# Dilated attention in halves of four heads between projections, and latent prompt attention with V stationary and probabilities scaled ahead of the turn

## The chip, the cores and the metric

The kernel runs on one core of one Trainium2 chip. The metric is the device time of one execution in microseconds, the median of several runs. Everything is computed in 32-bit floats, so each matrix multiplication shows as two passes (MATMUL records) on TensorE, and a turn (transpose by the identity) as one.

## The reference, cut to what matters

One step of a decoder trunk with two layers, for a prompt of 1024 tokens and for 8 new tokens that each have 8192 cached positions. The first layer mixes with latent attention and gated linear attention, the second with dilated attention; each is followed by a SwiGLU FFN, and each sublayer by a LayerNorm. The change is in the prompt part of the latent attention and in the whole of the dilated attention.

```
def mla_attend(q_lat, q_pe, kv, q_pos):               # latent attention, 8 heads, causal
    s = (q_lat . c_kv + q_pe . k_pe) * (64 + 32) ** -0.5
    p = softmax(where(k_pos <= q_pos, s, -inf))
    return p . c_kv                                    # then times w_uv: 64 values a head

def odd_mixer(x, bufs, w_in, w_out):                   # 3 groups (window, dilation) x 8 heads x 64
    qkv = x @ w_in
    for g, (window, dil) in enumerate(((128, 1), (512, 4), (2048, 16))):
        o_g, lse_g = attention in blocks of 128 positions of equal residue, with ALiBi bias
        rows_g = last window rows of k and v           # an output of its own
    w = softmax over the three groups of lse_g         # for each position and head
    return (sum_g w_g * o_g) @ w_out
```

For the 8 new tokens the dilated attention takes 128 cached keys and values a group (every dil-th row) and the token's own.

## The kernel before, in words

All activations live transposed in SBUF: X holds 8 tiles of 128 features by 1032 tokens, cut into three chunks of 344 (C) for the projections. Weights come in tiles through two slots (`slot`), loaded by SP's queue. The engines PE (TensorE), ACT (ScalarE), DVE (VectorE) and SP each run one stream of instructions in the order in which the program issues them, and wait for each other by counting semaphores; nothing else orders the work. `enter` and `leave` are barriers between some stages.

**Latent prompt attention** (`pe_mla`, `act_mla`, `dve_mla`, lines 1292 to 1438). `MU` lists 64 units, head by head, each a block of 128 queries against n = 1 to 8 blocks of 128 keys, in the order 1, 8, 2, 7, 3, 6, 4, 5. PE makes the keys of a head (`keys`, 8 passes of 512 columns), the scores of a unit into two banks (`scores`), turns the probabilities into banks 4 and 5 (`turn`), and multiplies them with V (`values`): the turned probabilities stand still and 64 columns of V move. DVE adds the causal mask and takes the maximum in one operation (`mask`, L1407), negates it (L1410), inverts the sum (L1419) and copies the turned probabilities out (`finish`, L1424). ACT takes the exponential in place with its sum (L1378), and scales the 128 x 64 result by the inverse as it copies it to O (`output`, L1374). Probabilities are in two buffers SP_, the turned ones in one, PT. PE issues scores(u+1), turn(u), values(u-1); DVE mask(u+1), finish(u); ACT the exponential of u, output(u-2). Last, O is turned into MO, the input of the output projection (L1362).

**Dilated attention.** For each group g in the order 0, 1, 2 there is dense work (`pe_dense`: 8 tiles of queries and keys in 24 steps, L1821; 18 steps of V rows, L1832; then turns of the key rows that are an output, L1841), and 16 attention units, each a block of 128 queries and four heads (`hq`), against one or two blocks of keys: 15 key blocks over the 8 query blocks in group 0, 12 in group 1, 8 in group 2. A unit is `pe_scores` (L1967), `dve_mask` (L2026 adds the bias, L2031 takes the maximum, L2034 scales it), `act_soft` (four exponentials with sums, L2007), `pe_turn` (L1979), `dve_turned` (L2043), `pe_values` (L1995), `act_output` (L2013). The output, maxima and sums of a block go by POOL's queue to `scratch_o` in memory. `with_dense` spreads the units of group g-1 between the dense steps of group g, so dense work of group 0 runs alone, then group 1's with the attention of group 0, group 2's with that of group 1; and `alone` runs the 16 units of group 2 at the end. After a barrier, `*_combine` reads the three groups back 128 positions at a time, weighs and adds them (L2092 to L2107), turns the sum into MX (L2131), and between these does the cached keys (`pe_decode_queries` spreads a query over 128 partitions, L2206; `dve_decode_scores` multiplies, L2195, and sums, L2198). After a second barrier, `*_dil_decode` does the softmax over the cached scores and the cached values (L2266, L2270). After a third, the output projection (`pe_proj`, L382) runs in three chunks of 8 tiles, with the LayerNorm of a chunk (L304, L308, L312 to L335, L344 to L352) between the tiles of the next, and the second FFN starts.

Of the kernel before, what the change touches and what calls it, by code (L numbers as in the profile page):

```python
# [23 lines left out]
P = 128  # L24
# [41 lines left out]
def build(nc, io):  # L66
    ctx = ExitStack()
    with ctx:
# [298 lines left out]
        def sp_out_c(sp):  # L367
            sp.wait_ge(e_sc, 2)
            for u in range(2):
                sp.dma_start(W_OUTC[:, u],  # L370
                             io["w_out_c"][u:8:2].rearrange("m p w -> p m w")).then_inc(loaded[u], 16)

        def pe_proj(pe, n_ln, lb, tb, kt, rhs, after_sum, after_var, whole=False, evicted=None, more=None):
            for s, (c, n) in enumerate(STEPS):
                u = s % 2
                if evicted is not None:
                    evicted(s)
                pe.wait_ge(loaded[u], 16 * (lb // 2 + 1 + (0 if whole else s // 2)))
                pe.wait_ge(free[u], 3 * (tb // 2) + s // 2 + 1)
                w = W_OUTC[:, u, n // 2, :].rearrange("p (k n) -> p k n", k=kt) if whole else w_tiles(u, kt)  # L380
# [828 lines left out]

        KVROW = [at(A_TMP + NH * T + q * KVD, KVD) for q in range(2)]  # L1210
# [52 lines left out]
        o = A_TMP + NH * T  # L1263
        KH = [at(o + q * SEQ, SEQ) for q in range(2)]; o += 2 * SEQ
        assert o <= A_END
        SP_ = [at(A_PB + T_CQ * T + q * SEQ, SEQ) for q in range(2)]
        PT = at(A_PB + T_CQ * T + 2 * SEQ, SEQ)
        O = at(A_PB + T_GQ * T, NT, 512)
        o = A_CONST + CONST_SIZE - 64
        m_max, m_neg, m_sum, m_inv = (at(o + 2 * q, 2) for q in range(4))  # L1270
# [5 lines left out]
        MU = [(h, i) for h in range(NH) for i in QORDER]  # L1276
# [14 lines left out]

        def pe_mla(pe):
            def keys(h):

                if h >= 2:
                    pe.wait_ge(m_tc, NT * (h - 1))
# [4 lines left out]
                mm.then_inc(kh_ps, 1)  # L1301

            def scores(u):
                h, i = MU[u]
                if u % NT == 0:
                    pe.wait_ge(kh_cp, h + 1)
                if h < 2 and u % NT == 0:
                    pe.wait_ge(kh_pe, 2)
# [3 lines left out]
                for c in range(0, nk, 512):  # L1312
                    w = min(512, nk - c)
                    mm = pe.matmul(ps[:, 2 * (u % 2) + c // 512, 0:w], QH[0:96, h, i * P:(i + 1) * P],
                                   KH[h % 2][0:96, c:c + w], start=True, stop=True)
                mm.then_inc(m_s, 1)

            def turn(u):
                h, i = MU[u]
                pe.wait_ge(m_p, u + 1)  # L1320
                if u % NT == 0:
                    pe.wait_ge(kh_cp, h + 2 if h + 1 < NH else h + 1)
                if u:
                    pe.wait_ge(m_tc, u)
                for j in range(i + 1):
                    mm = pe.transpose(ps[:, 4 + j // 4, (j % 4) * P:(j % 4) * P + P], SP_[u % 2][:, j * P:(j + 1) * P],
# [3 lines left out]
            def values(u):  # L1330
                h, i = MU[u]
                pe.wait_ge(m_tc, u + 1)
                if u == 0:
                    pe.wait_ge(v_cp, NT)
                if u >= 2:
                    pe.wait_ge(m_oc, u - 1)
                for j in range(i + 1):
                    mm = pe.matmul(ps[:, 6 + u % 2, 0:64], PT[:, j * P:(j + 1) * P], V[:, j, h * 64:h * 64 + 64],
                                   start=(j == 0), stop=(j == i))
                mm.then_inc(m_o, 1)  # L1340

            keys(0)
            for u, (h, i) in enumerate(MU):
                if u == 0:
                    scores(0)
                    pe.wait_ge(kh_cp, 1)
                    keys(1)
                if u + 1 < len(MU):
                    scores(u + 1)
                turn(u)  # L1350
                if u:
                    values(u - 1)
                if u % NT == NT - 1 and h + 2 < NH:
                    keys(h + 2)
            values(len(MU) - 1)
            pe.wait_ge(m_oc, len(MU))

            for tt in range(NT):
                if tt >= 4:
                    pe.wait_ge(mo_c, tt - 3)  # L1360
                for f in range(4):
                    mm = pe.transpose(ps[:, tt % 4, f * P:(f + 1) * P], O[:, tt, f * P:(f + 1) * P], ident[:, :])  # L1362
                mm.then_inc(mo_t, 1)
            leave("pe", pe)

        mo_t, mo_c = sem("mo_t"), sem("mo_c")
        MO = at(A_END - 4 * T, 4, T)

        def act_mla(act):
            def output(u):  # L1370
                h, i = MU[u]
                act.wait_ge(m_o, u + 1)
                act.wait_ge(m_iv, u + 1)
                act.mul(O[:, i, h * 64:h * 64 + 64], ps[:, 6 + u % 2, 0:64], m_inv[:, u % 2:u % 2 + 1]).then_inc(m_oc, 1)  # L1374

            for u, (h, i) in enumerate(MU):
                act.wait_ge(m_ng, u + 1)
                act.activation(SP_[u % 2][:, 0:(i + 1) * P], SP_[u % 2][:, 0:(i + 1) * P], ACT.Exp,  # L1378
                               bias=m_neg[:, u % 2:u % 2 + 1], scale=MLA_SCALE,
                               accum_out=m_sum[:, u % 2:u % 2 + 1]).then_inc(m_p, 1)  # L1380
                if u >= 2:
                    output(u - 2)
            output(len(MU) - 2)
            output(len(MU) - 1)
            act.wait_ge(m_oc, len(MU))
# [4 lines left out]
        def dve_mla(dve):  # L1390
            for q in range(2):
                dve.wait_ge(row_out[q], 16 * (NT // 2))
            for q in range(2):
                dve.tensor_copy(KH[q][64:96, :], PB[64:96, T_MISC, 0:SEQ]).then_inc(kh_pe, 1)
            def keys(h):
                dve.wait_ge(kh_ps, h + 1)
                dve.tensor_copy(KH[h % 2][0:64, :].rearrange("p (c t) -> p c t", c=2), ps[0:64, 4:6, :]).then_inc(kh_cp, 1)

            def mask(u):
# [3 lines left out]
                if u >= 2:  # L1403
                    dve.wait_ge(m_t, u - 1)
                    dve.wait_ge(m_p, u - 1)
                pv = ps[:, 2 * (u % 2):2 * (u % 2) + 2, :].rearrange("p a b -> p (a b)")[:, 0:nk]
                dve.tensor_tensor_reduce(SP_[u % 2][:, 0:nk], pv, causal[:, SEQ - nk:SEQ], 1.0, NEG, ALU.add, ALU.max,  # L1407
                                         m_max[:, u % 2:u % 2 + 1]).then_inc(m_mask, 1)
                dve.wait_ge(m_mask, u + 1)
                dve.tensor_scalar(m_neg[:, u % 2:u % 2 + 1], m_max[:, u % 2:u % 2 + 1], -MLA_SCALE, None,  # L1410
                                  ALU.mult).then_inc(m_ng, 1)

            def finish(u):
                h, i = MU[u]
                nk = (i + 1) * P
                dve.wait_ge(m_p, u + 1)
                if u >= 2:
                    dve.wait_ge(m_oc, u - 1)
                dve.reciprocal(m_inv[:, u % 2:u % 2 + 1], m_sum[:, u % 2:u % 2 + 1]).then_inc(m_iv, 1)  # L1419
                dve.wait_ge(m_t, u + 1)  # L1420
                if u >= 1:
                    dve.wait_ge(m_o, u)
                pv = ps[:, 4:6, :].rearrange("p a b -> p (a b)")[:, 0:nk]
                dve.tensor_copy(PT[:, 0:nk], pv).then_inc(m_tc, 1)  # L1424

            keys(0)
            mask(0)
            keys(1)
            for u, (h, i) in enumerate(MU):
                if u + 1 < len(MU):  # L1430
                    mask(u + 1)
                finish(u)
                if u % NT == NT - 1 and h + 2 < NH:
                    keys(h + 2)
            for tt in range(NT):
                dve.wait_ge(mo_t, tt + 1)
                dve.tensor_copy(MO[:, :, tt * P:(tt + 1) * P], ps[:, tt % 4, :].rearrange("p (f t) -> p f t", f=4)).then_inc(mo_c, 1)
            dve.wait_ge(mo_c, NT)
# [4 lines left out]
        GW = GP * KVD  # L1443
# [288 lines left out]

        o = A_L
        QK = [at(o + q * 8 * T, 8, T) for q in range(2)]; o += 16 * T
        A_CACHED = A_L + 8 * T + 104
        VB = [at(o + (1 - q) * (NT + 1) * 512, NT + 1, 512) for q in range(2)]; o += 2 * (NT + 1) * 512
        A_LATE = o - (NT + 1) * 512
        BIAS = at(o, NH, 2 * P); o += NH * 2 * P
        DS = [at(o + q * 4 * 2 * P, 4, 2 * P) for q in range(2)]; o += 16 * P
        DPT = [at(o + q * 4 * 2 * P, 4, 2 * P) for q in range(2)]; o += 16 * P  # L1740
        OW = 512 + 2 * NH
        OG = [at(o + q * OW, OW) for q in range(2)]; o += 2 * OW
        KROW = [at(o + q * 512, 512) for q in range(2)]; o += 1024
        DMX = at(o, 2, 4); o += 8
        assert o <= A_END, o
        QS, VS = at(A_CONST + 2 * P, 3, 512), at(A_CONST + 2 * P + 1536, 3, 512)
        KS1 = at(A_DEC0, 512)

# [8 lines left out]

        bias_in = sem("bias_in")
        k_ps, k_cp, k_zero, s_in, vb_out = sem("k_ps"), sem("k_cp"), sem("k_zero"), sem("s_in"), sem("vb_out")
        krow_out = [sem("krow_out0"), sem("krow_out1")]  # L1760
# [13 lines left out]
        def kept_blocks(groups):  # L1774
            return sum(len(kept_list(g)) for g in range(groups))

        def key_units(g):

            return [(blk, 4, P) for blk in kept_list(g)] + [(NT, 4, DEC), (NT, 0, DEC)]

        def k_before(g):
# [909 lines left out]
```

## Time and profile before

| | us |
|---|---|
| median of 3 runs | 3705.65 (3702.84 to 3706.67) |
| the profiled execution | 3705.62 |
| its span in the trace | 3703.5 |
| PE busy | 3427.2 (93%) |
| PE weight loads busy | 2516.6 (68%) |
| DVE busy | 1728.4 (47%) |
| ACT busy | 607.5 (16%) |

[...]

### The profile page before, as it was taken

How to read it: one execution, taken by the hardware profiler on the slowest of the kernel's cores; microseconds unless marked ns; L12 is line 12 of the kernel's file. 1: busy time of each engine (PE TensorE's matmuls, PEld its weight loads, DVE VectorE, ACT ScalarE, POOL GpSimd, SP SyncE). 2: the span in 40 equal slices, each digit the busy share in tenths (PEclk: the TensorE clock that was granted, in tenths of full speed). 3: DMA queues.
4: the chain of work that ended last, by engine and by line, in shares of the span. 5: the costliest groups of instructions: out<-in, count | busy, mean ns of one | idle time of the engine just before them, and what ended most of it. 6: DMA issues, size and time to landing. Idle time of an engine off the chain costs nothing. (4 is left out here: it accounts for less than half of the span.)

```text
span 3703.5 us, 44517 instructions
## 1 busy us (share of the span) xinstructions
PE 3427.2 (93%) x18200; PEld 2516.6 (68%) x18200; DVE 1728.4 (47%) x3623; ACT 607.5 (16%) x1534; POOL 45.4 (1%) x63
## 2 busy tenths in 40 slices
PE   9999899776989999999999999998768999999997
PEld 5675466554657777776867779688525777777677
DVE  1216455677254333367740233124556443335777
ACT  1214133233120000000120111112203100000002
POOL 0000000010000000000000000000000000000000
PEclk9999799899999999999999999998569999999998
DMA  3120200488311111111311111113410101111122
GB/s 132 34 57 1 77 1 1 180 334 308 97 57 57 37 42 45 45 63 63 103 63 40 35 49 47 47 38 131 146 47 23 46 34 45 45 45 59 63 77 109
DMA packets 61670, 270.85 MB, mean 73 GB/s; under 512 B 5584, under 2 KB 17368, under 8 KB 50112
## 3 DMA queue, kind: packets, MB, share of 16 engines
q1 hardware_dynamic: 54544, 183.43, 14.3%
q0 software_dynamic: 6960, 85.14, 6.0%
q8 instruction: 113, 1.85, 0.2%
q14 instruction: 53, 0.43, 0.0%
HBM read 248.45 MB, written 20.10 MB: 73 GB/s over the span
## 5 line engine op out<-in xcount | busy, mean ns | idle before, releaser
L520 PE MATMUL ps<-arena 128*128 128x344 f32 (+1 forms) x4928 | 1082.6, 383 | 20.0 <-ACT arena L561 12.0
L520 PEld LDWEIGHTS ps<-arena 128*128 128x128 f32 x4928 | 832.5, 191 | 271.2 <-issue 30.3
L769 PE MATMUL ps<-arena 128*128 128x344 f32 (+1 forms) x2464 | 539.5, 381 | 1.5 <-DVE arena L688 1.5
L769 PEld LDWEIGHTS ps<-arena 128*128 128x128 f32 x2464 | 414.6, 190 | 127.2 <-DVE arena L688 3.4
L1821 PE MATMUL ps<-arena 128*128 128x344 f32 x1152 | 345.8, 459 | 7.4 <-ACT arena L352 5.7
L1821 PEld LDWEIGHTS ps<-arena 128*128 128x128 f32 x1152 | 218.5, 192 | 120.7 <-issue 11.5
L216 PE MATMUL ps<-arena 128*128 128x344 f32 x672 | 199.2, 460 | 8.9 <-DMA arena<-in_w_a 8.9
L1832 PE MATMUL ps<-arena 128*128 128x256 f32 (+1 forms) x864 | 207.1, 397 | 0.0
L1832 PEld LDWEIGHTS ps<-arena 128*128 128x128 f32 (+1 forms) x864 | 179.7, 263 | 21.5 <-issue 3.3
L216 PEld LDWEIGHTS ps<-arena 128*128 128x128 f32 x672 | 129.7, 193 | 77.6 <-DMA arena<-in_w_a 8.9
L563 ACT ACTIVATE arena<-arena 128x688 f32<-128x688 f32 (+1 forms) x88 | 55.7, 633 | 756.7 <-DVE arena L625 756.7
L1659 DVE STREAM_TRANSPOSE arena<-arena 128x1152 f32<-128x1152 f32 x128 | 167.2, 1351 | 21.9 <-DMA arena<-in_cache,arena 21.9
L382 PE MATMUL ps<-arena 128*128 128x344 f32 x576 | 174.5, 465 | 2.6 <-issue 1.7
L382 PEld LDWEIGHTS ps<-arena 128*128 128x128 f32 x576 | 112.3, 196 | 62.9 <-issue 6.8
L2007 ACT ACTIVATE arena<-arena 128x128 f32<-128x128 f32 (+1 forms) x192 | 84.1, 439 | 344.7 <-DVE arena L2034 344.7
L1533 PE MATMUL ps<-arena 128*32 128x128 f32 x2304 | 82.2, 305 | 55.7 <-DVE arena L1659 55.7
L1857 DVE COPY arena<-ps 128x344 f32<-128x344 f32 x36 | 18.5, 516 | 219.4 <-PE ps L1821 219.3
L1533 PEld LDWEIGHTS ps<-arena 128*32 128x32 f32 x2304 | 71.4, 123 | 64.7 <-DVE arena L1659 63.3
L599 DVE TENSOR_TENSOR arena<-arena 128x512 f32<-128x512 f32 x44 | 30.4, 691 | 151.6 <-DMA arena<-in_w_fi 151.6
L1864 DVE COPY arena<-ps 128x256 f32<-128x256 f32 (+1 forms) x54 | 22.8, 423 | 160.1 <-PE ps L1832 160.1
L2026 DVE TENSOR_TENSOR arena<-ps,arena 128x256 f32<-128x256 f32 (+1 forms) x96 | 48.0, 541 | 105.7 <-PE ps L1967 75.0
L625 DVE TENSOR_TENSOR arena<-arena,ps 128x344 f32<-128x344 f32 (+1 forms) x88 | 37.2, 422 | 109.0 <-PE ps L520 109.0
(312 smaller groups left out, 3578.2 us busy)
## 6 DMA issues: line engine op xcount, KB each, us to landing
arena<-in_w_fi SPq DMA_DIRECT2D x44, 1024.0 KB, 4.8
arena<-in_w_fo SPq DMA_DIRECT2D x16, 1536.0 KB, 6.3
arena<-in_w_fo SPq DMA_DIRECT2D x16, 1280.0 KB, 5.7
arena<-in_w_out_a SPq DMA_DIRECT2D x24, 512.0 KB, 3.5
arena<-in_w_qk SPq DMA_DIRECT2D x24, 512.0 KB, 3.5
arena<-in_c SPq DMA_DIRECT2D x5, 2048.0 KB, 12.7
arena<-in_x SPq DMA_DIRECT2D x6, 1376.0 KB, 10.2
arena<-in_w_a SPq DMA_DIRECT2D x14, 512.0 KB, 3.5
```

Source lines behind the costliest of these rows:

```text
L216: mm = pe.matmul(ps[:, 3 * u + c, 0:C], w[:, k, :], X[:, k, chunk(c)], start=(k == 0), stop=(k == KD - 1))
L382: mm = pe.matmul(ps[:, 3 * u + s // 2 % 3, 0:C], w[:, k, :], rhs(k)[:, chunk(c)], start=(k == 0), stop=(k == kt - 1))
L520: mm = pe.matmul(ps[:, BANK[p], 0:HALF[s]], prod[j][p][0], prod[j][p][1], start=(j == 0), stop=(j == 3))
L563: act.activation(GATE[:, 0:2 * HALF[s]], GATE[:, 0:2 * HALF[s]], ACT.Silu).then_inc(st_g, 1)
L625: dve.tensor_tensor(GATE[:, h:2 * h], x, bank["p3"], ALU.add).then_inc(st_e, 1)
L769: mm = pe.matmul(ps[:, BANK[p], 0:HALF[s]], prod[p][0], prod[p][1], start=(j == 0), stop=(j == NKP - 1))
L1533: mm = pe.matmul(ps[32 * j:32 * j + 32, n % 2, 0:P], QBD[n // NG % 2][:, cb, :], KVT[(4 * n + j) % 8][:, :, cb * 32:cb * 32 + 32], start=( ...
L1659: dve.transpose(KVT[(4 * n + q) % 8], KV[n % 4][:, 4 * q:4 * q + 4, :]).then_inc(kt_done, 1)
L1821: mm = pe.matmul(ps[:, b, 0:C], w[:, k, :], X[:, k, chunk(c)], start=(k == 0), stop=(k == KD - 1))
L1832: mm = pe.matmul(ps[0:P if tt < NT else DEC, b, 0:256], X[:, k, block_slice(g, tt)], w[:, k, :], start=(k == 0), stop=(k == KD - 1))
L2007: act.activation(DS[u % 2][:, j, 0:nk], DS[u % 2][:, j, 0:nk], ACT.Exp, bias=DMX[:, u % 2, j:j + 1], scale=DIL_SCALE, accum_out=OG[blk % 2 ...
L2026: dve.tensor_tensor(DS[u % 2][:, a::2, 0:nk], ps[:, dil_bank(g, u, a), :].rearrange("p (b k) -> p b k", k=2 * P)[:, :, 0:nk], BIAS[:, 4 * ...
```

## The change

**Latent prompt attention.** `MU` now goes by pairs of heads: (h, i), (h+1, i), with the same order of i. There are four SP_, four KH and two PT. A new ACT step `norm` scales the whole block of probabilities by the inverse sum before the turn (semaphore m_n); `values` takes both heads of a pair at once, with 64 columns of V standing still for each and 128 columns of the turned probabilities moving, into partitions 0 to 63 and 64 to 127 of one bank. `output` is a plain copy straight to MO, and the turn of O is gone.

```diff
-        MU = [(h, i) for h in range(NH) for i in QORDER]
+        MU = [(h, i) for hp in range(0, NH, 2) for i in QORDER for h in (hp, hp + 1)]
...
             def turn(u):
                 h, i = MU[u]
-                pe.wait_ge(m_p, u + 1)
-                if u % NT == 0:
-                    pe.wait_ge(kh_cp, h + 2 if h + 1 < NH else h + 1)
+                pe.wait_ge(m_n, u + 1)
+                pe.wait_ge(kh_cp, made[0])
                 if u:
                     pe.wait_ge(m_tc, u)
...
+                for j in range(i + 1):
+                    for q in range(2):
+                        mm = pe.matmul(ps[64 * q:64 * q + 64, 6 + w % 2, 0:P], V[:, j, (h + q) * 64:(h + q) * 64 + 64],
+                                       PT[q][:, j * P:(j + 1) * P], start=(j == 0), stop=(j == i))
...
+            scores(0)
+            scores(1)
+            for u, (h, i) in enumerate(MU):
+                turn(u)
+                if u + 2 < len(MU):
+                    scores(u + 2)
+                if u % 2:
+                    values(u // 2)
+                if u % 16 in KEYS_AT and h + 2 < NH:
+                    keys(h - h % 2 + 2 + KEYS_AT[u % 16])
...
+            def norm(u):
+                h, i = MU[u]
+                act.wait_ge(m_iv, u + 1)
+                act.mul(SP_[u % 4][:, 0:(i + 1) * P], SP_[u % 4][:, 0:(i + 1) * P], m_inv[:, u % 4:u % 4 + 1]).then_inc(m_n, 1)
...
+            soft(0)
+            soft(1)
+            norm(0)
+            for u in range(len(MU)):
+                if u + 2 < len(MU):
+                    soft(u + 2)
                 if u + 1 < len(MU):
...
+                    norm(u + 1)
+                if u % 2 and u > 1:
+                    output(u // 2 - 1)
...
             for u, (h, i) in enumerate(MU):
+                if u + 2 < len(MU):
+                    mask(u + 2)
                 if u + 1 < len(MU):
-                    mask(u + 1)
+                    inverse(u + 1)
                 finish(u)
```

**Dilated attention.** The work is cut into six halves (group, four heads), in the order of groups 1, 2, 0. A half has 12 dense steps of queries and keys, 9 of V rows, the turns of its key rows, and 8 attention units. Projections use banks 6 and 7, from the second half on two deep. The attention of half i-1 runs between the dense steps of half i; only the last half's runs without any (`pe_last`, `act_last`, `dve_last`). Groups 1 and 2 go through `scratch_o`; group 0's two halves keep their output, and are joined with the other two unit by unit (`dve_stats`, `act_weights`, `dve_weights`, `act_output`, `dve_joined`, `pe_joined`, `act_joined`), the reads of `scratch_o` being POOL's. The cached keys of groups 1 and 2 are multiplied during halves 2 and 4, those of group 0 in the last stage, with the softmax over them. The first chunk of the output projection stands among the last units (`FIRST_CHUNK`), the cached values between its second and third chunk. The three barriers are gone.

```diff
+        GORD = (1, 2, 0)
+        HALVES = [(g, hq) for g in GORD for hq in range(2)]
...
+        def pe_last(pe):
+            for it in range(NU + 4):
+                if it < NU:
+                    pe_scores(pe, 5, it)
+                if it < 4:
+                    pe_query(pe, 2, 2 * it, 6)
+                    pe_query(pe, 2, 2 * it + 1, 7)
...
+                if 1 <= it <= NU:
+                    pe_turn(pe, 5, it - 1)
+                if 2 <= it < NU + 2:
+                    pe_values(pe, 5, it - 2)
+                if it >= 4:
+                    pe_joined(pe, 5, it - 4)
+                for n in FIRST_CHUNK.get(it, ()):
+                    pe_out_c(pe, 0, n)
+            for n in range(8):
+                pe_out_c(pe, 1, n)
...
+            pe_decode_values(pe, 0)
+            pe_ln_sum(pe, 2, 1)
+            pe_decode_values(pe, 1)
+            pe_decode_values(pe, 2)
+            pe_ln_var(pe, 2, 1)
+            pe_decode_turn(pe)
+            for n in range(8):
+                pe_out_c(pe, 2, n)
...
+        def pe_out_c(pe, c, n):
...
+            if n == 0:
+                pe.wait_ge(c_tc, NU + (3, 6, 8)[c])
+            if c == 2 and n == 0:
+                pe.wait_ge(e_tc, 4)
...
+            dve_out_c_sum(dve, 1)
+            dve_ln_centre(dve, 2, 1)
+            dve_ln_squares(dve, 2, 1)
+            dve_ln_scale(dve, 2, 1)
+            dve_decode_copy(dve)
+            dve_decode_out(dve)
+            dve_t_in(dve, 2, 0, range(2))
+            dve_out_c(dve, 2, 0)
+            dve_out_c(dve, 2, 1)
+            dve_t_in(dve, 2, 0, range(2, 4))
+            for n in range(2, 8):
+                dve_out_c(dve, 2, n)
+            dve_out_c_sum(dve, 2)
...
             dve_w_in(dve, l, 0)
-            if l:
-                dve_t_in(dve, n_ln, 0, range(4))
             dve_ln_centre(dve, n_ln, 2)
```

## Rows read from the trace of the kernel before

**Rows 1.** Busy time by stage: window, its length, engines' busy time (instructions), clock, DMA.
```profile
448.00:682.00 234.00, 207.74 (x1152) 140.24 (x1152) 127.76 (x338) 70.37 (x192) 2.51 (x2) 0.97 0.05 21
...
1884.00:2069.00 185.00, 179.03 (x687) 127.28 (x688) 27.82 (x41) 15.84 (x25) 0.56 (x1) 0.98 0.12 40
2069.00:2310.00 241.00, 239.91 (x1267) 190.40 (x1266) 75.95 (x116) 42.78 (x154) 4.34 (x8) 1.00 0.12 42
2310.00:2550.00 240.00, 237.53 (x1083) 185.95 (x1082) 59.37 (x107) 36.83 (x141) 3.78 (x7) 0.99 0.12 41
2550.00:2660.00 110.00, 84.52 (x469) 74.44 (x469) 49.36 (x99) 35.90 (x162) 5.92 (x11) 0.59 0.41 150
2660.00:2726.00 66.00, 35.07 (x68) 14.89 (x67) 54.92 (x107) 5.68 (x16) 0.00 (x0) 0.63 0.56 196
2726.00:2770.00 44.00, 31.08 (x124) 6.29 (x123) 14.29 (x26) 0.71 (x2) 0.00 (x0) 0.58 0.00 0
2770.00:2832.00 62.00, 59.81 (x198) 38.63 (x197) 31.71 (x38) 15.88 (x17) 0.00 (x0) 0.96 0.02 3
```

**Rows 2.** Timeline of latent prompt units: start, duration, engine, line, operation [idle before].
```profile
559.51 1.08 PE L1314 MATMUL ps<-arena 96*128 96x512 f32 x2
...
560.49 0.85 PE L1326 MATMUL ps<-arena 128*128 128x128 f32 x6
560.63 0.69 DVE L1407 CUSTOM_DVE_ANT_0 arena<-ps,arena 128x512 f32<-128x512 f32 x1 [0.29 <-PE ps L1314]
...
561.36 0.15 DVE L1410 TENSOR_SCALAR arena<-arena 128x1 f32<-128x1 f32 x1
561.55 0.72 ACT L1378 ACTIVATE arena<-arena 128x512 f32<-128x512 f32 x1 [1.44 <-DVE arena L1410]
...
562.18 0.19 ACT L1378 ACTIVATION_READ_ACCUMULATOR arena<-arena 128x1 f32 x1
...
563.63 1.45 PE L1338 MATMUL ps<-arena 128*128 128x64 f32 x12
```

**Rows 3.** Groups by line and shape, whole span: count, busy us, mean ns, idle before.
```profile
L1407 DVE CUSTOM_DVE_ANT_0 arena<-ps,arena 128x1024 f32<-128x1024 f32 x8 | 9.8, 1224 | 5.8 <-PE ps L1314 5.8
L1424 DVE COPY arena<-ps 128x1024 f32<-128x1024 f32 x8 | 9.8, 1225 | 7.9 <-PE ps L1338 7.9
L1378 ACT ACTIVATE arena<-arena 128x1024 f32<-128x1024 f32 x8 | 9.2, 1148 | 56.6 <-DVE arena L1410 56.6
L1378 ACT ACTIVATE arena<-arena 128x512 f32<-128x512 f32 x8 | 5.8, 721 | 11.6 <-DVE arena L1410 11.6
L2026 DVE TENSOR_TENSOR arena<-ps,arena 128x512 f32<-128x512 f32 x44 | 28.4, 686 | 50.3 <-PE ps L1967 50.3
L312 DVE TENSOR_TENSOR arena<-arena 128x1376 f32<-128x1376 f32 x24 | 38.1, 1589 | 8.8 <-ACT arena L344 8.2
L335 DVE TENSOR_TENSOR arena<-arena 128x2752 f32<-128x2752 f32 x12 | 36.3, 3026 | 51.0 <-ACT arena L349 51.0
```

**Rows 4.** Passes into column groups: a group by shape, then one row of the timeline.
```profile
L1533 PE MATMUL ps<-arena 128*32 128x128 f32 x2304 | 82.2, 305 | 55.7 <-DVE arena L1659 55.7
...
2742.44 1.89 PE L2266 MATMUL ps<-arena 128*8 128x512 f32 x8 [0.70 <-DVE arena L2230]
```

**Rows 5.** Timeline: score passes over 128 columns, then key passes over 64.
```profile
454.30 0.49 PE L1314 MATMUL ps<-arena 96*128 96x128 f32 x2 [1.31 <-DVE arena L1397]
454.72 3.65 PE L1299 MATMUL ps<-arena 128*64 128x512 f32 x8
```

**Rows 6.** Busy time in two slices of 10 us, dilated group alone and joining.
```profile
2600.00:2610.00 10.00, 8.50 (x45) 7.68 (x44) 4.80 (x11) 3.83 (x18) 0.54 (x1) 0.50 0.09 33
...
2690.00:2700.00 10.00, 4.36 (x11) 2.26 (x12) 9.33 (x20) 0.70 (x2) 0.00 (x0) 0.66 0.25 83
```

**Rows 7.** The first group's dense stretch, L1821 alone and L1832 alone (PE, weight loads).
```profile
1884.00:2069.00 185.00, 114.50 (x384) 74.19 (x384) 0.98 0.12 40
...
1884.00:2069.00 185.00, 62.72 (x288) 51.27 (x288) 0.98 0.12 40
```

**Rows 8.** DMA issues of the cached keys and values: size of one, median us to landing.
```profile
arena<-in_c SPq DMA_DIRECT2D x5, 2048.0 KB, 12.7
```

More of the change, by code:

```diff
@@ L1340, in values @@
                 mm.then_inc(m_o, 1)
             keys(0)
+            pe.wait_ge(kh_cp, 1)
+            keys(1)
+            scores(0)
+            scores(1)
             for u, (h, i) in enumerate(MU):
[L1344 to L1349, printed above, removed]
-                turn(u)
[L1351 to L1354, printed above, removed]
@@ L1772, in kept_list @@
             return [blk for blk in range(NT) if kept(g, blk) is not None]
[L1774 to L1781, printed above, removed]
-            return kept_blocks(g) + 3 * g
-        TILES, D_KEYS = 3 * 8, 3 * 8 + ROWS
-        def dense_steps(g):
-            return D_KEYS + len(key_units(g))
-        def dense_tile(g, d):
-            return QK_FIRST[d] if g == 0 and d < 6 else divmod(d, 3)
@@ L1842, in pe_dense @@
[L1842 to L1852 removed]
+                    for e in range(TILES - 6, TILES):
+                        dense_done(pe, i, e)
@@ new lines, in pe_values, with pe_joined, act_soft @@
+            mm.then_inc(a_o, 1)
+        def pe_joined(pe, i, u):
+            v = NU * (i - 4) + u
+            pe.wait_ge(c_row, v + 1)
+            if v:
+                pe.wait_ge(c_tc, v)
+            for f in range(2):
+                mm = pe.transpose(ps[:, 5, f * P:(f + 1) * P], CO[v % 2][:, f * P:(f + 1) * P], ident[:, :])
+            mm.then_inc(c_t, 1)
+        def act_soft(act, i, u):
+            g, n, nk = unit(i, u)
+            s = stat(i, u)
+            act.wait_ge(a_ng, n + 1)
+            stat_free(act, i, u)
+            for j in range(4):
+                act.activation(DS[n % 2][:, j, 0:nk], DS[n % 2][:, j, 0:nk], ACT.Exp, bias=DMX[:, n % 2, j:j + 1],
+                               scale=DIL_SCALE, accum_out=s[:, 260 + j:261 + j]).then_inc(a_p, 1)
@@ new lines, in act_weights, with act_output @@
+        def act_weights(act, i, u):
+            v = NU * (i - 4) + u
+            act.wait_ge(c_m, v + 1)
+            act.activation(CE[v % 2], CE[v % 2], ACT.Exp, scale=DIL_SCALE).then_inc(c_e, 1)
+        def act_output(act, i, u):
+            n = NU * i + u
+            act.wait_ge(a_o, n + 1)
+            if i < 4:
+                act.copy(OG[n % 3][:, 0:256], ps[:, 4, 0:256]).then_inc(a_oc, 1)
+            else:
+                v = n - 4 * NU
+                act.wait_ge(c_w, v + 1)
+                for j in range(4):
+                    ins = act.activation(OR[v % 4][:, 0, 64 * j:64 * j + 64], ps[:, 4, 64 * j:64 * j + 64], ACT.Copy,
+                                         scale=CE[v % 2][:, 0, j:j + 1])
+                ins.then_inc(a_oc, 1)
@@ new lines, in with_dense @@
+        def with_dense(i, dense, scores, turn, values, joined, rows, decode):
+            total, d, n_it = dense_steps(i), 0, NU + (4 if i > 4 else 2)
+            for it in range(n_it):
+                while d < 2 + (total - 2) * 2 * it // (2 * n_it):
+                    dense(i, d)
+                    d += 1
+                if it < NU:
+                    scores(i - 1, it)
+                while d < 2 + (total - 2) * (2 * it + 1) // (2 * n_it):
+                    dense(i, d)
+                    d += 1
+                if 1 <= it <= NU:
+                    turn(i - 1, it - 1)
+                if 2 <= it < NU + 2:
+                    values(i - 1, it - 2)
+                if i > 4 and 3 <= it < NU + 3:
+                    joined(i - 1, it - 3)
+                if i > 4 and it >= 4:
+                    rows(i - 1, it - 4)
+                if i in (2, 4):
+                    decode(i // 2 - 1, it)
+            while d < total:
+                dense(i, d)
+                d += 1
```

1095 lines of the change are left out of this document (569 added, 526 removed).

## The prediction

> **What bounds the kernel now.** I read the table of busy time by stage first [rows 1]. TensorE is the bound wherever projections run: it is busy for 240 of 241 us in the stretch in which one dilated group is projected and the one before it attends. Three kinds of stretch are not like that: the latent prompt attention (208 busy of 234 us), the last dilated group alone (84.5 of 110, at a granted clock of 0.59), and the joining of the groups with the cached keys and values (35 of 66 and 31 of 44 us, clock 0.63 and 0.58). The change touches just these. Then I read the timeline of one latent unit [rows 2] and the durations by shape [rows 3], because both edits turn on orders of waits rather than on amounts of work.
>
> **Part 1, latent prompt attention: TensorE's work.** A unit is one head and one block of 128 queries with n key blocks, n = 1 to 8, 64 units and 288 blocks in all. Before, values take 12 passes in 1.45 us, 0.12 a pass [rows 2], 576 passes: 70 us. After, V (64 columns) stands still and 128 columns of turned probabilities move; heads h and h+1 use column groups 0 and 1. Alone that is 0.107 us a pass like a turn; if both groups run at once, 0.053. The trace has such groups: 2304 passes of 32 columns in 82.2 us, 0.036 each, and eight 512-column passes in 1.89 us at half clock, where one alone takes 0.85 [rows 4]. I take 0.053: 31 us, so 39 us less TensorE work; without overlap, 61 us. The final turn of O (32 passes, 6.5 us to the end of its copies) goes.
>
> **Part 1, the order of the waits.** Before, the loop issues scores(u+1), turn(u), values(u-1): TensorE always has scores and values in hand while mask and exponential run. After, it issues turn(u), scores(u+2), values, and turn(u+1) waits for the new norm(u+1) (m_n). ScalarE runs soft(u+2) and only then norm(u+1), and soft(u+2) waits for mask(u+2), which waits for scores(u+2), which stands behind turn(u). So one unit's period is the whole ring turn(u), scores(u+2), mask(u+2), m_neg, soft(u+2), norm(u+1), turn(u+1). The four SP_ buffers don't help: no two links of it overlap. VectorE's finish(u) stands behind mask(u+2) and inverse(u+1) too, beside the ScalarE part.
>
> Price of the ring at full clock. From the first score pass of a unit of n = 4 (559.51) to the end of its exponential's sum (562.37) is 2.86 us [rows 2]; its part that grows is 0.213 scores, 0.134 mask (1.224 us at 1024, 0.69 at 512) and 0.107 exponential (1.148 at 1024, 0.721 at 512) a block [rows 2, 3], so 1.82, and 1.05 is fixed. The norm is a ScalarE pass over the same tile, for which I take the exponential's slope and its fixed part without the accumulator: 0.29 + 0.107n. The turn is 0.107n (six in 0.85 with the tail [rows 2]) and about 0.15 of waits. Sum: 1.49 + 0.668n. Over 64 units: 95 + 192 = 288 us.
> Added to it: six times keys(h) falls between values and turn(u+1), which now waits for kh_cp: 3.65 us of passes [rows 5] and a copy of 1024, 1.22 us [rows 3], of which the ring hides part, 28 us. Where a pair of many blocks is followed by one of few, finish(u) and values outlast soft and norm: 2.0, 1.5, 1.2 us a head pair, 19 us. Start and tail 14 us. Together 349 us against 234 before. That is +115, the lower end.
>
> The clock is the second term. In this ring TensorE has about 1.9 us of columns in 5.4 us, 36%. The nearest rows are the dilated group alone: 8.5 us busy of 10, that is 42% at full rate, and its clock stays at 0.50 for 50 us; in the joining stage, 4.36 of 10 busy, it goes up and down with a mean of 0.66 [rows 6]. At half clock turn and scores add 0.32n a unit, 92 us, keys 29, the values that stick out 25: 495 us, the upper end (+261). The ring has long bursts, at keys and at values(8) followed by turn and scores(7), that should bring the clock back for some us each; I take 70% of that extra, 100 us: about 450 us, **+216 us**.
>
> Switching to column groups has a price of its own: after 128-column score passes the 64-column key passes start 0.42 us later instead of 0.21 [rows 5]. Two switches a head pair's unit, 32 units, would be 13 us, but most fall where TensorE waits anyway, so I add nothing. [...]
>
> **Part 2, dilated attention.** Before, from the first projection to the end of the output projection: 1884 to 2832, 948 us [rows 1].
> After, dense work is unchanged: a group is 114.5 + 62.7 us [rows 7], three are 531. Attention beside it costs (241 + 240) - 2 x 177 = 127 us for the 1080 passes of groups 0 and 1, 0.117 a pass. The new order (1, 2, 0 in halves) leaves only half of group 0, 300 passes, for the end, so 1100 of 1400 passes stand beside projections: 129. Cached queries move under them too, 16 x 2 passes of 512 columns, 14 us; turns of the first joined half 3; the 6 us idle at the start stays; 7 more for waits on VectorE (KROW behind its DMAs, one bank fewer for projections). 690 us.
> The last half alone is VectorE's: per unit two adds of 0.686, a maximum over 1024 and the turned copy of 1024, 1.22 each [rows 3], the scale 0.17, seven small ones of about 0.18 (the smallest is 0.15 [rows 2]) 1.25, four of 256 elements at 0.42 1.7, waits 0.4: 7.4 us, eight are 59. Beside them eight key products of 512 at 0.69, one key sum over 4096, 4.4, the cached softmax in ten small ones 3.8, eight evictions of 344 at 0.51: 18; these go by their size at the rows' slope. Filling, draining and the first output tile's wait for c_tc, 13, and a low clock for part of it 8: 98 us (85 to 125, where TensorE at half clock becomes the bound).
> What moves between queues: the cached keys, 2 MB and 12.7 us each [rows 8], go out on SP between the weights of halves 1, 3 and 5. The next half's first tiles stand behind them, but nine V steps of 16 passes at 0.213 (31 us) cover that. The reads of scratch_o move from SP to POOL, a third of the size and three units ahead of a 7 to 10 us period. Uncovered they would cost one such landing each, some 10 us, which the ends hold. Cached values follow a_o 5*NU and e_sc 3 on SP and land under the alone stretch.
> Output projection after that: chunk 1, 8 tiles of 8 passes at 0.287, 18 us, 22 with LN steps of 3.0 us [rows 3] between evictions from two banks; then pe_out_c of chunk 2 waits for e_tc 4, and in front of it VectorE has scale, sum, centre, squares, scale (3 us each), ScalarE's part of the norm, OE's copy, the turn and eight small copies: 28 us, over TensorE's 22 us of cached values (twelve runs of eight passes, 1.89 us each at half clock [rows 4]); chunk 2, 22. Sum 690 + 98 + 22 + 28 + 22 = 860, so -88 us. dve_t_in leaves the start of the second FFN, four additions of 1376, 1.59 each [rows 3]: -6. **-94 us**. The ends: with-projection part 690 or 715, alone 85 or 125, then 19 or 26, 22 or 32 and 20 or 26: -118 and -30.
>
> **Sum.** 3705.6 (span 3703.5 and 2.1 around it, equal to the median of the runs) + 216 - 94 = **3828 us**.
>
> **Rivals.**
> A, *the look-ahead works*: four SP_ buffers and two units ahead hide the chain and TensorE is the bound. Then the stage keeps its 26 us of idle and loses 36 to 39 us of values and 7 of the last turn, about 190 us, -43; with -94: 3569. For it: buffers and the halved values. Against: scores(u+2) is issued behind turn(u), and norm(u+1) behind soft(u+2). It decides from the point at which norm(u+1) can run before soft(u+2); the order of issue never lets it.
> B, *the ring, but the clock holds*: 349 us, 3727. For: the stage before holds 0.97. Against: there TensorE is 89% busy.
> C, *low clock all along or the gain of part 2 lost*: 495 us gives 3873; with 450 and only -30 in part 2, 3892. For: the alone stage never recovered in 50 us. Against: key bursts.
> D, *the two parts cancel*: +115 and -118, 3703, within what I call no change.
>
> **How the numbers follow.** Forecast (clock mixed, stage 400 to 480 us, part 2 between -60 and -118) 0.50, B 0.17, C 0.18, A 0.12, D 0.03. Likeliest 3828. The range takes in B and most of C and leaves out A, D and C's tail, 0.19: 3715 to 3905. 0.2%, 7.4 us, is what can be told from no change here: faster 0.12 (A), same 0.03 (D), slower 0.85.
>
> **What would show it.** Right: in the latent stage every turn is preceded by an idle TensorE released by ScalarE's norm, about 5 to 7 us a unit, the same in ScalarE's waits for m_neg; granted clock there well under 0.9; about 450 us in all. Values: pairs of passes under 0.06 us each at full clock. Part 2: one alone stretch of about 100 us with VectorE over 75% busy, TensorE over 98% busy before it. Wrong: a unit period near 3 us (A), or a clock above 0.9 with the ring (B).

## The result and the profile after

The changed kernel takes 3869.93 us, median of 4 runs (3868.51 to 3872.11), against 3704.24 (3699.38 to 3706.67) for the kernel before: ratio 1.045, 95% interval 1.0431 to 1.0468. It is 166 us slower; 3828 was forecast, in a range of 3715 to 3905. The profiled execution has a span of 3870.3 us.

Busy time by stage in the kernel after, as in [rows 1]: the latent stage, the dilated attention with projections, its last half alone, and the end up to the second FFN's first pass.

```profile
449.00:892.00 443.00, 284.32 (x1157) 167.01 (x1161) 119.63 (x338) 103.09 (x224) 3.28 (x3) 0.62 0.03 11
2087.00:2830.00 743.00, 713.64 (x3254) 540.57 (x3255) 212.17 (x419) 132.06 (x479) 29.12 (x50) 0.98 0.17 58
2830.00:2925.00 95.00, 67.81 (x378) 50.64 (x377) 64.44 (x153) 27.49 (x113) 2.84 (x4) 0.78 0.30 102
2925.00:3015.00 90.00, 71.60 (x262) 33.54 (x260) 47.07 (x55) 21.82 (x27) 0.00 (x0) 0.80 0.06 24
```

The latent stage went from 234 to 443 us at a mean granted clock of 0.62, full clock being 1.00. VectorE and ScalarE have about the work they had plus the norm; TensorE's busy time rose from 207.74 us (1152 passes) to 284.32 (1157) because many passes are slower: four turn passes (L1318) take 0.63 us at 552.96, where the clock is 1.00, and 1.12 at 564.27, where it is 0.50. From the stage's end to the first query projection it is 1196 us (892 to 2087.75), before 1202 (682 to 1884.28), so that part 1 as a whole costs 203 us. From there to the first pass of the second FFN it is 927.4 us (to 3015.19), before 964.2 (to 2848.46): part 2 gives 37 us back.

TensorE's waits in the latent stage after: line that waits, line waited for, us in total, times, longest.

```profile
PE ps L1318 <- ACT arena L1365: 89.7, 38, 3.1
PE ps L1331 <- DVE arena L1423: 56.3, 32, 1.9
```

One turn of the ring in the timeline after (L1307 scores, L1406 mask, L1409 m_neg, L1358 exponential, L1365 norm, L1318 turn). The scores, mask and exponential are those of unit u+2, of one key block; the norm and the turn are those of unit u+1, of five. It answers to [rows 2].

```profile
565.39 0.64 PE L1307 MATMUL ps<-arena 96*128 96x128 f32 x2
566.06 0.29 DVE L1406 CUSTOM_DVE_ANT_0 arena<-ps,arena 128x128 f32<-128x128 f32 x1 [3.76 <-PE ps L1307]
...
566.39 0.15 DVE L1409 TENSOR_SCALAR arena<-arena 128x1 f32<-128x1 f32 x1
...
566.58 0.40 ACT L1358 ACTIVATE arena<-arena 128x128 f32<-128x128 f32 x1 [3.11 <-DVE arena L1409]
...
566.98 0.81 ACT L1365 ACTIVATE arena<-arena 128x640 f32<-128x640 f32 x1
...
567.85 1.33 PE L1318 MATMUL ps<-arena 128*128 128x128 f32 x5 [1.82 <-ACT arena L1365]
...
568.97 0.64 PE L1307 MATMUL ps<-arena 96*128 96x128 f32 x2
```

Each line starts where the one above ends, within 0.1 us (the last but for 0.2): one unit from scores to scores, 3.58 us, and no two links of this path overlap. The idle time before the mask (3.76) and before the exponential (3.11) is the same ring seen from the other engines.

### The profile page after: what moved, and what is told of

The parts are those of the page before. It is cut to its first block and busy times, and to the rows that moved or that the text cites. A ratio compares the mean times of both kernels' runs of the same rounds, so it can differ in the third digit from the quotient of the medians.

```text
span 3870.3 us, 44575 instructions
## 1 busy us (share of the span) xinstructions
PE 3482.7 (90%) x18168; PEld 2526.8 (65%) x18168; DVE 1713.0 (44%) x3695; ACT 662.5 (17%) x1660; POOL 63.1 (2%) x90
## 5 line engine op out<-in xcount | busy, mean ns | idle before, releaser
L512 PEld LDWEIGHTS ps<-arena 128*128 128x128 f32 x4928 | 831.5, 191 | 264.5 <-issue 23.0
L759 PEld LDWEIGHTS ps<-arena 128*128 128x128 f32 x2464 | 414.6, 190 | 127.5 <-DVE arena L678 3.4
L1945 PE MATMUL ps<-arena 128*128 128x344 f32 x1152 | 352.3, 462 | 15.1 <-ACT arena L352 5.7
L1945 PEld LDWEIGHTS ps<-arena 128*128 128x128 f32 x1152 | 219.4, 193 | 134.0 <-issue 24.3
L216 PE MATMUL ps<-arena 128*128 128x344 f32 x672 | 198.1, 458 | 9.5 <-DMA arena<-in_w_a 9.5
L216 PEld LDWEIGHTS ps<-arena 128*128 128x128 f32 x672 | 129.2, 193 | 77.6 <-DMA arena<-in_w_a 9.5
L1406 DVE CUSTOM_DVE_ANT_0 arena<-ps,arena 128x128 f32<-128x128 f32 (+7 forms) x64 | 48.5, 758 | 267.8 <-PE ps L1307 267.7
L1318 PE MATMUL ps<-arena 128*128 128x128 f32 x288 | 72.0, 405 | 98.9 <-ACT arena L1365 89.7
L1318 PEld LDWEIGHTS ps<-arena 128*128 128x128 f32 x288 | 48.8, 203 | 135.0 <-ACT arena L1365 115.4
L1307 PE MATMUL ps<-arena 96*128 96x512 f32 (+3 forms) x192 | 121.3, 762 | 0.9 <-DVE arena L1396 0.9
L1331 PE MATMUL ps<-arena 128*64 128x128 f32 x576 | 69.4, 424 | 56.3 <-DVE arena L1423 56.3
L374 PE MATMUL ps<-arena 128*128 128x344 f32 x384 | 113.4, 457 | 0.8 <-DVEq L155 0.8
L1331 PEld LDWEIGHTS ps<-arena 128*64 128x64 f32 x576 | 56.7, 223 | 86.2 <-DVE arena L1423 86.2
L1531 PEld LDWEIGHTS ps<-arena 128*32 128x32 f32 x2304 | 69.9, 121 | 64.4 <-DVE arena L1657 63.2
## 6 DMA issues: line engine op xcount, KB each, us to landing
arena<-in_c SPq DMA_DIRECT2D x6, 2048.0 KB, 11.2
```

The costliest lines, as they stand in the source:

```text
L216: mm = pe.matmul(ps[:, 3 * u + c, 0:C], w[:, k, :], X[:, k, chunk(c)], start=(k == 0), stop=(k == KD - 1))
L512: mm = pe.matmul(ps[:, BANK[p], 0:HALF[s]], prod[j][p][0], prod[j][p][1], start=(j == 0), stop=(j == 3))
L759: mm = pe.matmul(ps[:, BANK[p], 0:HALF[s]], prod[p][0], prod[p][1], start=(j == 0), stop=(j == NKP - 1))
L1331: mm = pe.matmul(ps[64 * q:64 * q + 64, 6 + w % 2, 0:P], V[:, j, (h + q) * 64:(h + q) * 64 + 64], PT[q][:, j * P:(j + 1) * P], start=(j == ...
L1531: mm = pe.matmul(ps[32 * j:32 * j + 32, n % 2, 0:P], QBD[n // NG % 2][:, cb, :], KVT[(4 * n + j) % 8][:, :, cb * 32:cb * 32 + 32], start=( ...
L1945: mm = pe.matmul(ps[:, b, 0:C], w[:, k, :], X[:, k, chunk(c)], start=(k == 0), stop=(k == KD - 1))
```

## The experiments

Times are medians; in brackets the ratio to the kernel before with its interval.

**The two parts alone.** `part1_alone` is the kernel before with the new latent attention, `part2_alone` with the new dilated attention.

> The kernel before with only the new latent prompt attention. If the two parts are independent, it takes the 208 us that the latent stage got longer in the trace of the changed kernel (449 to 892 us against 448 to 682): 3704 + 208 = 3912 us. Rival: some of the 208 us is the other part's doing (other buffers, other loads under the stage); then clearly less than 3912, for example 3870 if the dilated part is worth nothing.

> The kernel before with only the new dilated attention. Independent parts: 3870 - 208 = 3662 us, that is 42 us faster than before and not the 94 us forecast. Rival: the long low-clock stage in front costs the later stages something, then 3640 or less; or the parts share a cost, then above 3680.

Measured 3904.13 us (1.0546, 1.0528 to 1.0564) and 3666.12 us (0.9904, 0.9888 to 0.9921), beside 3702.43: +202 and -36, where 3912 and 3662 were expected. They add up to the measured +166.

**The norm's place on ScalarE.**

```diff
             for u in range(len(MU)):
-                if u + 2 < len(MU):
-                    soft(u + 2)
                 if u + 1 < len(MU):
                     norm(u + 1)
+                if u + 2 < len(MU):
+                    soft(u + 2)
```

> The changed kernel with one swap on ScalarE: norm(u+1) ahead of soft(u+2). Ring theory: the exponential leaves the ring, the rest stays in it (scores(u+2) behind turn(u), inverse(u+1) behind mask(u+2)). It took 0.48 + 0.107n us a unit, 61 us over 64 units and 288 blocks; VectorE's copy and the values are late next in some units, so 45 to 61 us less: 3809 to 3825 us. Rival, TensorE's own work at a low clock is the bound of the stage: no change, 3865 to 3875.

Measured 3831.68 us (1.0357, 1.0339 to 1.0374), 38 us below after and 7 more than the upper end expected. TensorE's wait for the norm fell from 89.7 to 57.3 us; its wait for VectorE's copy, 56.3 before, did not move:

```profile
PE ps L1318 <- ACT arena L1365: 57.3, 33, 2.0
PE ps L1331 <- DVE arena L1423: 56.2, 32, 1.9
```

The clock rose only from 0.62 to 0.65 (449 to 852). The norm's place alone does not open the ring; mask(u+2) still stands behind turn(u).

**The clock by itself.** The kernel after, with unused passes of 384 columns in TensorE's idle time of the ring.

```diff
+            def filler(u):
+                n = [MU[q][1] + 1 for q in (u, u + 1, u + 2)]
+                gap = 1.28 + 0.241 * n[2] + 0.107 * n[1] - (0.213 * n[0] + 0.2 if u % 2 else 0)
+                if u >= 4:
+                    pe.wait_ge(m_oc, u // 2 - 1)
+                for _ in range(int(max(0, gap - 0.3) / 0.64)):
+                    pe.matmul(ps[:, 6 + u // 2 % 2, 128:512], ident[:, :], causal[:, 0:384], start=True, stop=True)
...
                     scores(u + 2)
+                    filler(u)
```

> The changed kernel with 170 extra multiplications of 384 columns (two passes each, 109 us at full clock), put behind scores(u+2) and sized to the idle time of TensorE in the ring; their result is not used. Theory, the ring is set by waits and TensorE's idle time lowers the clock, which costs the ring 0.32n us a unit: the clock rises above 0.9 and the latent stage goes from 442 to about 355 us, in all 3783 us (3775 to 3810) although 109 us of work were added. Rival, TensorE's work is the bound: 109 to 180 us longer, 3980 or more. Rival, the clock stays low whatever stands in the gaps: about 3900, since fillers at half clock outlast them.

Measured 3783.27 us (1.0212, 1.0193 to 1.0232): 87 us faster with 109 us more work. Busy time in the latent stage, which now ends at 803:

```profile
449.00:682.00 233.00, 196.11 (x911) 110.64 (x911) 77.58 (x217) 65.91 (x144) 2.58 (x2) 0.94 0.05 21
682.00:803.00 121.00, 103.75 (x579) 63.42 (x582) 40.41 (x117) 37.12 (x82) 0.21 (x1) 0.94 0.00 1
```

The order of issue is that of after, so the ring is the same; at a granted clock of 0.94 it takes 354 us in place of 443. The clock alone is worth 89 us, the ring at nearly full clock the other 120 over the 234 of before. The filling passes can also hold the ring up, so 89 us is rather too little than too much.

**Breaking the ring.** `scores_first` moves one line on TensorE; `scores_and_norm_first` adds the ScalarE diff above.

```diff
             for u, (h, i) in enumerate(MU):
-                turn(u)
                 if u + 2 < len(MU):
                     scores(u + 2)
+                turn(u)
```

> The kernel after, with TensorE's scores(u+2) ahead of turn(u) in the latent stage and nothing else moved. My theory: the period of 443 us is a ring over one unit, closed by the order of issue alone. With the scores ahead, the loop turn(u+1), scores(u+4), mask, exponential, norm spans two units, half of 1.49 + 0.668n, and TensorE's own work (the stage before, 233 us, less 39 for the values and 7 for the last turn) becomes the bound: 190 to 210 us at a granted clock over 0.9, so the whole 3870 - 240 = about 3630. Rival 1, the norm's place behind the next exponential is the real limit: 260 to 300 us, 3690 to 3730. Rival 2, switching between tiles of 64 and 128 columns or the finish on VectorE limits it: idle before L1331 or L1307 stays at 50 us or more, 250 us, 3680.

> As scores_first, and on ScalarE norm(u+1) ahead of soft(u+2). My theory: with the scores ahead the norm's place costs little, so 5 to 15 us less than scores_first: about 3620. If the norm's place were the real limit, this one would be 50 us or more below scores_first. If TensorE bounds both, they are equal within 5 us.

Measured 3698.49 us (0.9988, 0.9977 to 0.9998) and 3672.03 us (0.9923, 0.9905 to 0.9942). One moved line is worth 171 us, which settles that the ring was made by the order of issue. Both are slower than expected (3630, 3620). The first lies in rival 1's range: its latent stage takes 270 us (449 to 719) at a clock of 0.86, and TensorE waits 28.7 us for the norm and 27.2 for the copies in front of the values, so that rival 2, with 50 us or more in front of L1331 or L1307, is out. The norm's place is then worth 26 us, more than my 5 to 15 and less than the 50 that would make it the limit, and the latent stage of the second kernel still takes 244 us (449 to 693), not 190 to 210. TensorE's waits in 449:690 of the second name what is left:

```profile
PE ps L1331 <- DVE arena L1423: 34.4, 31, 1.3
PE ps L1318 <- ACT arena L1365: 9.2, 21, 1.0
```

The values of a pair stand directly behind the turn of its second unit and wait for that unit's copy, 31 times. In the forecast, finish and values that outlast the ring were 19 us at full and 44 at half clock; in after this wait is 56.3 us.

**The values one unit later.** On top of the last kernel, three PT and three SP_ in place of two and four, and the keys of the next pair one unit later.

```diff
-                if u % 2:
-                    values(u // 2)
+                if u % 2 == 0 and u:
+                    values(u // 2 - 1)
```

> scores_and_norm_first (3672, latent stage 242 us) with the values of a pair one unit later, behind the turn of the next pair's first unit, three buffers in place of two for the turned probabilities and three in place of four for the scores. There TensorE waited 34.4 us for VectorE's copy of the unit just turned, right before the values. Theory: these waits are idle by the order alone, so 25 to 35 us go: latent stage 210 to 217, the whole 3640 to 3647, and the new attention is then about 20 us faster than the one before. Rival: VectorE and ScalarE take over (a period of mask, copy and small ones, or of exponential and norm), the wait moves to L1318 behind ScalarE's norm: 3662 to 3672.

Measured 3644.27 us (0.984, 0.9824 to 0.9857), as expected. The stage, 449 to 664, and one run of values in it:

```profile
449.00:664.00 215.00, 180.95 (x1118) 105.77 (x1116) 117.11 (x330) 103.10 (x224) 1.75 (x2) 0.95 0.06 23
...
643.33 1.75 PE L1331 MATMUL ps<-arena 128*64 128x128 f32 x28
```

215 us against 234: with the same instructions as in after, in another order and with the buffers shared out otherwise, the new attention is the faster one, and the clock is 0.95. Part of the wait did move on, to the turn behind the norm (25.1 us, 18 times, longest 2.2).

**The strides.** In `part2_no_strides` every block of tokens is 128 tokens in a row, so each query meets other keys; the instructions and their shapes stay.

```diff
-            return slice(s, s + (P - 1) * d + 1, d)
+            return slice(blk * P, blk * P + P)
```

> The kernel with only the new dilated attention (3666), but every block of tokens read as 128 tokens in a row in place of every 4th or 8th (another set of keys for each query, so another result; same instructions, same shapes). My sum took the strided groups at the price of rows without strides. Theory: the stride is paid on TensorE, scores of the strided groups 0.16 in place of 0.08 us a pass and V steps 4.0 in place of 3.5 us, and it is paid in full now that all of groups 1 and 2 stand beside projections: 25 us of scores, 18 of V steps, 3 of key turns, so 3666 - 45 = about 3620. Rival: the strides cost nothing and the 52 us that the part took over my 690 are waits and switches between tile shapes: then 3655 to 3668.

Measured 3629.2 us (0.9804, 0.9783 to 0.9825), 37 us below `part2_alone`, where 45 were expected. A unit's scores, 8 passes for one block and 16 for two, in the kernel after (every 4th token, then every 8th)

```profile
2202.71 1.30 PE L2042 MATMUL ps<-arena 64*128 64x128 f32 x8
...
2408.80 2.42 PE L2042 MATMUL ps<-arena 64*128 64x128 f32 x16
...
2571.91 1.32 PE L2042 MATMUL ps<-arena 64*128 64x128 f32 x8
```

and without strides:

```profile
2173.36 1.26 PE L2034 MATMUL ps<-arena 64*128 64x128 f32 x16
...
2337.55 0.71 PE L2034 MATMUL ps<-arena 64*128 64x128 f32 x8
```

A run of 16 V passes goes from about 4.1 to 3.65 us (4.20 and 3.97 against 3.72 and 3.62). Group 1's scores under projections are 8 units of 8 passes and 8 of 16, group 2's 16 units of 8: 8 x 0.6 + 8 x 1.16 + 16 x 0.6 = 24 us, and 32 V runs by 0.4 are 13: 37 us, the measured gain. The cost of strides is shown; that it explains my miss is not, see below. It is there in full at a stride of 4 (1.30 us for 8 passes, against 0.71) and no larger at 8 (1.32).

**The waits of part 2.** On top of `part2_alone`; besides what is shown, one weight load waits for five tiles in place of six, and in the last half TensorE's queries and turned scores go behind the turn.

```diff
             for it in range(n_it):
+                if i in (2, 4):
+                    early(i // 2 - 1, it)          # dve_decode; it was the iteration's last
...
             for half in range(2):
+                if k == 2 and half:
+                    pe_ln_var(pe, 2, 1)            # was behind all cached values
...
-            dve_ln_scale(dve, 2, 1)
             dve_decode_copy(dve)
             dve_decode_out(dve)
+            dve_ln_scale(dve, 2, 1)
```

> The kernel with only the new dilated attention (3666), with orders changed: VectorE's product with the cached keys ahead of the iteration's copies, one weight load's wait one tile earlier, in the last half alone TensorE's queries and turned scores behind the turn, and at the end the second chunk's variance pass between the last cached values and VectorE's scale behind the cached outputs. If the waits read in the trace are real: 11 + 4 us while projections run, 8 to 12 in the last half alone, 7 at the end, so 3666 - 32 = about 3634. If they only move to another link: 3655 or more.

Measured 3629.81 us (0.9809, 0.9788 to 0.983), 36 us below `part2_alone`, where 32 were expected, all of it orders. These rows are TensorE's waits from 1884 to 2830 in `part2_alone` (L2235 is the query, L2243 the product, L2329 the turn of the cached outputs, L2268 that of the scores, the last row the late weight load):

```profile
PE ps L2235 <- DVE arena L2243: 22.7, 17, 5.0
PE ps L2329 <- DVE arena L2323: 6.7, 1, 6.7
...
PE ps L2268 <- DVE arena L2247: 5.6, 1, 5.6
...
PE ps L1937 <- DMA arena<-in_w_qk: 3.8, 1, 3.8
```

and these the same waits in `part2_orders`; the third and the last are gone, while a turn's wait for VectorE's copy grows from 0.4 to 5.5 us:

```profile
PE ps L2237 <- DVE arena L2245: 7.3, 3, 2.5
...
PE ps L2045 <- DVE arena L2128: 5.5, 1, 5.5
...
PE ps L2333 <- DVE arena L2327: 1.4, 1, 1.4
```

**Both together.** `all_orders` is `values_later` with the edits of `part2_orders`.

> values_later together with the orders of part2_orders. If the parts add: 3629.8 for part2_orders with the attention before, and the latent stage 16 to 23 us below the 233 before: 3607 to 3614, the fastest so far. Rival: the latent gain of values_later does not come, then 3630 to 3640.

Measured 3603.86 us (0.9733, 0.9717 to 0.9749): 3 us below the expected range, 2.7% faster than the kernel before, and 266 us faster than the kernel after. It is the fastest version.

## Why the prediction was right, point by point

**The order of the waits: right.** The ring was forecast from the order of issue and is in the timeline link by link. It is not closed by the norm in every unit, though, as my sign of being right had it: all 32 turns that stand right behind scores wait for the norm, but of the other 32, most of them behind values, only 6 do. Before those, TensorE has already waited for VectorE's copy (56.3 us), which stands behind the same mask, so the path goes there through the copy and the values and no longer through the exponential and the norm. Its size at full clock, 349 us, has its counterpart in 354 at a clock of 0.94 with the filling passes. Rival A, the look-ahead, fell for the reason given (scores(u+2) issued behind turn(u)): with that line moved, units overlap. Its stage of 190 us came in no run; 215 in `values_later` is the nearest. It decides at the scores, though, and not at the place of the norm that I had named for it: moving the norm alone gave 38 us, the scores alone 171.

**The clock: right in kind and size.** 100 us were taken, 89 are shown; 0.62 granted. The nearest row used, TensorE's load in the dilated group alone [rows 6], pointed the right way. 450 us for the stage, 443 measured; +216 forecast, +202 as `part1_alone` against its own kernel before. Half of that difference of 14 is the stage; 6 us lie behind it (1196 in place of 1202) and were in no term. At least in part they are the clock's, which came back sooner there: 0.83 from 1139 to 1149, against 0.50 at the same point of the kernel before (930 to 940). Rival B (clock holds) fell by the same row, C's half clock all along too. That a burst brings the clock back, and the 70% of the extra, were estimates of mine. In the kernel after TensorE is busy without a gap from 545.2 to 551.6 us, with values and then keys, and the granted clock is 1.00 from 549 to 555; with values, turn and scores it is busy from 842.8 to 849.0, and the clock is 1.00 from 849 to 851, when TensorE waits again and gains nothing by it.

**Values in column groups: they overlap**, 28 passes in 1.75 us at full clock, 0.063 a pass against 0.053 taken, "under 0.06" in my signs, and 0.12 before [rows 2]. It is 5 us off on 576 passes, and not worth anything where the ring is the bound. The price of switching to column groups, taken as nothing, was not measured by itself.

**The step that failed: part 2's size**, forecast -94, measured -36 alone and -37 in the trace of after; rival C had -30 as its end. By terms:
- With projections 690 forecast, 743 measured. Idle TensorE was taken as 13 us (6 + 7) and is 29: the queries wait 11.2 us for VectorE's product, the third weight load comes 3.7 late, and the rest was in the 13 or is small. TensorE was 96% busy, not over 98%. These are the waits in the kernel after:

```profile
PE ps L2243 <- DVE arena L2251: 11.2, 14, 2.3
...
PE ps L1945 <- DVE arena L2007: 4.0, 1, 4.0
PE ps L1945 <- DMA arena<-in_w_qk: 3.7, 1, 3.7
```

- The other 37 us are busy time. Two terms are in these rows of after, the queries, priced too low, and the key row turns, whose growth I had left out: the three stretches of before have 38 key row passes in 5.7 us:

```profile
L2243 PE MATMUL ps<-arena 128*128 128x512 f32 x34 | 19.3, 648 | 11.2 <-DVE arena L2251 11.2
L1966 PE MATMUL ps<-arena 128*128 128x128 f32 x52 | 10.4, 312 | 1.7 <-DVE arena L2007 1.7
L1969 PE MATMUL ps<-arena 128*8 128x128 f32 x24 | 4.0, 294 | 0.7 <-DVE arena L2007 0.7
```

  Key row turns in halves are 76 passes in 14.4 us, 9 more; the queries are 19.3 in place of 14. Behind the key sum the granted clock falls to 0.87 from 2440 to 2480, and over the whole part it is 0.98 against 0.98, 1.00 and 0.99 in [rows 1]: 5 to 10 us by my estimate. My expectation of `part2_no_strides` said that strides were the miss. They cost 37 us, but my rate of 0.117 a pass came from stretches that held group 1's strided scores and two groups' strided V steps already; new under projections are only group 2's scores, 16 x 0.6 = 10 us. 9 + 5 + 5 to 10 + 10 make 29 to 34 of the 37; the rest stays open.
- The last half alone: 98 forecast, 95 measured, but VectorE was 68% busy (64.4 of 95), not over 75%: two turns and the scores' turn stood behind queries on TensorE, which waited 11.7 us for VectorE's product, and the scores' turn 5.6 for its sum. At 2925 two tiles of the first output chunk are still to come, so by the forecast's own cut this stage takes 102 us.
- The end: 72 forecast (22 + 28 + 22), 84 measured from 2925. 7 of the 12 are those two tiles; the second chunk takes 21.4 us (2932.41 to 2953.79) and the third 21.2. The middle, 34.4 in place of 28, is what failed: the cached values took about the 22 priced (2953.79 to 2976.39), but the variance pass stands behind all of them, so ScalarE's step, VectorE's scale, the copy, the turn and eight small copies come one after another. In `part2_orders` the stretch from ScalarE's squares (L344) to the first pass of the third chunk is 16.1 us in place of 23.2. These rows of after show it (L308 variance pass, L335 scale, L2331 copy, L2337 turn, L2375 output projection):

```profile
2932.41 4.89 PE L2375 MATMUL ps<-arena 128*128 128x344 f32 x16 [0.61 <-DVE arena L2381]
...
2970.03 0.52 DVE L314 TENSOR_TENSOR arena<-arena 128x344 f32<-128x344 f32 x1
...
2976.39 1.52 PE L308 MATMUL ps<-arena 128*128 128x344 f32 x2
...
2980.39 3.02 DVE L335 TENSOR_TENSOR arena<-arena 128x2752 f32<-128x2752 f32 x1 [9.84 <-ACT arena L349]
2983.34 1.22 DVE L2331 COPY arena<-ps 128x1024 f32<-128x1024 f32 x1
...
2984.61 1.97 PE L2337 MATMUL ps<-arena 128*128 128x128 f32 x8 [6.70 <-DVE arena L2331]
...
2988.17 2.06 PE L2375 MATMUL ps<-arena 128*128 128x344 f32 x3 [1.59 <-DVE arena L2346]
```

  The squares' sum is done at 2970.55 and used at 2976.39, 5.8 us later.

- dve_t_in out of the second FFN's start: -6 forecast. From the output projection's end to the FFN's first pass it was 16 us (2832 to 2848.46) and is 6 (3009.4 to 3015.19).

The forecast of 3828 was 42 us too low, and the range held it because part 1, the large term, was right: part 2's miss (-94 against -36, 58) less part 1's (+216 against +202, 14) is 44, and the kernel before came out 1.4 lower than its first median.

## What to carry to other kernels

Buffers two units ahead help only if the orders of issue on each engine let two units overlap: write the period as a walk over the links (each engine's queue is one) and see whether any link of the next unit can start before this one closes. Here one line moved on one engine was worth 171 us, and three moves made a change that lost 4.5% win 1.6%. In this stage a wait chain on TensorE was charged twice: the ring took 354 us at a granted clock of 0.94 (`filler_passes`), against 234 before, and 443 at 0.62. And a rate taken from a mixed stretch must be taken apart (strides, block counts, key turns) before it is used on another mix.

## What the runs showed of the hardware that was not expected

- 109 us of unused passes in a stage that waits made the whole kernel 87 us faster, at a granted clock of 0.94 in place of 0.62.
- Score passes with both operands at a stride of 4 or 8 fp32 take 1.30 to 1.32 us for 8 (the kernel after), against 0.71 contiguous (`part2_no_strides`); both strides cost the same.
- Two column groups of 64 with 128 moving columns overlap almost fully: 0.063 us a pass at full clock (28 in 1.75, `values_later`), 0.12 at half clock (16 in 1.98, the kernel after at 562.36); full overlap would be 0.053 by my estimate, half of the 0.107 taken from the turn passes (six in 0.85 [rows 2]).
